# Turning half of the normalized token tiles by transposing DMAs instead of by TensorE in a hybrid decoder trunk

## The reference

```
for l in range(2):
    h = rms_norm(x, attn_pre_g[l])               # the "pre" norm
    u = h @ w_in[l]                              # 1024 -> 2560, split among four mixers
    y = concat(conv(u..), retention(u..), moba(u..), pool(u..)) @ w_out[l]
    x = x + rms_norm(y, attn_post_g[l])
    h = rms_norm(x, ffn_pre_g[l])                # the "fpre" norm
    f = silu(h @ w_gate[l]) * (h @ w_up[l])      # 1024 -> 2816, twice
    x = x + rms_norm(f @ w_down[l], ffn_post_g[l])
```

## Time and profile before

| what | us |
|---|---|
| median of 3 runs | 1102.46 (1101.63 to 1146.96) |
| the profiled execution | 1102.11 |
| its span | 1100.0 |
| PE busy | 1082.0 (98%) |
| DVE busy | 619.2 (56%) |
| ACT busy | 405.7 (37%) |
| transfers of DMA queue q1 | 31.2% of 16 engines |

### The profile page before, as it was taken

How to read it: one execution, slowest core, us unless ns; L and a number is a source line. 1 busy time by engine, 2 the same in 40 slices (tenths; PEclk the granted TensorE clock), 3 DMA queues, 4 the chain that set the end, 5 groups by cost and what they waited for, 6 DMA issues and landing times.

```text
span 1100.0 us, 15518 instructions
## 1 busy us (share of the span) xinstructions
PE 1082.0 (98%) x6086; PEld 601.9 (55%) x6086; DVE 619.2 (56%) x1419; ACT 405.7 (37%) x810; POOL 5.2 (0%) x18
## 2 busy tenths in 40 slices
PE   8999999999999999999999999999999999999997
PEld 4755784695444444444466558648844444444443
DVE  6998898873332432321568889989633433432014
ACT  5545445453332332221235463456522322321000
POOL 1000000000000000000000000000000000000000
PEclk9999999999999999999999999999999999999999
DMA  8423213254324323323013331234523333232001
GB/s 312 149 77 111 82 40 115 70 178 137 112 82 151 113 80 114 115 84 108 1 39 107 101 101 39 63 110 136 176 93 115 114 98 115 89 103 77 1 20 57
DMA packets 58167, 109.56 MB, mean 100 GB/s; under 512 B 7024, under 2 KB 7280, under 8 KB 57968
## 3 DMA queue, kind: packets, MB, share of 16 engines
q1 hardware_dynamic: 58096, 108.58, 31.2%
HBM read 106.46 MB, written 2.10 MB: 99 GB/s over the span
## 4 chain that ended last, share of the span: by engine, by line
PE 95%; DVE 3%; DMA 1%; issue 1%; ACT 0%; SPq 0%; ACTq 0%; DVEq 0%
PE ps L517 88%; PE ps L521 3%; PE ps L714 1%; PE ps L730 1%; DVE E L1302 1%; DMA xs<-x_dram 1%; PE ps L649 0%; DMA raw<-weights_dram 0%; PE ps L691 0%; PE ps L634 0%; DVE ring L1173 0%; ACT gbc L800 0%; PE ps L658 0%; PE ps L652 0%; PE ps L711 0%
## 5 line engine op out<-in xcount | busy, mean ns | idle before, releaser
L517 PE MATMUL ps<-hT,ring 128*128 128x512 f16 (+1 forms) x3264 | 547.9, 329 | 0.0
L517 PEld LDWEIGHTS ps<-hT,ring 128*128 128x128 f16 x3264 | 319.0, 98 | 223.0
L517 PE MATMUL ps<-ring,U 128*128 128x512 f16 x1440 | 313.4, 379 | 0.0
L1173 DVE SCALAR_TENSOR_TENSOR ring<-raw,ring 128x512 f16<-128x512 f32 x368 | 230.1, 684 | 80.6 <-ACT ring L800 79.8
L800 ACT ACTIVATE ring<-raw 128x512 f16<-128x512 f32 x368 | 205.5, 621 | 109.0 <-PE ps L517 78.7
L517 PEld LDWEIGHTS ps<-ring,U 128*128 128x128 f16 x1440 | 140.9, 98 | 167.0
L1497 DVE SCALAR_TENSOR_TENSOR R<-ps,R 128x512 f32<-128x512 f32 (+1 forms) x52 | 31.7, 609 | 257.6 <-ACT R L976 257.2
L517 PE MATMUL ps<-ring,hT 128*128 128x512 f16 x576 | 133.2, 383 | 0.7 <-DVE hT L1262 0.7
L976 ACT ACTIVATE R<-ps 128x512 f32<-128x512 f32 (+1 forms) x52 | 27.6, 530 | 277.9 <-PE ps L517 277.9
L1302 DVE SCALAR_TENSOR_TENSOR E<-E,par 128x256 f32<-128x256 f32 x240 | 101.9, 477 | 0.1
L517 PEld LDWEIGHTS ps<-ring,hT 128*128 128x128 f16 x576 | 56.2, 99 | 62.0 <-issue 3.0
(11 more groups left out here) (109 smaller groups left out, 494.9 us busy)
## 6 DMA issues: line engine op xcount, KB each, us to landing
raw<-weights_dram SPq DMA_DIRECT2D x368, 256.0 KB, 3.3
gbc<-gains_dram SPq DMA_DIRECT2D x8, 512.0 KB, 5.5
xs<-x_dram SPq DMA_DIRECT2D x4, 512.0 KB, 6.6
U<-weights_dram SPq DMA_DIRECT2D x8, 256.0 KB, 7.6
out_dram<-xs SPq DMA_DIRECT2D x8, 256.0 KB, 2.0
cst<-consts_dram SPq DMA_DIRECT2D x1, 1296.0 KB, 12.3
bd<-pool_w_dram SPq DMA_DIRECT2D x8, 16.0 KB, 10.1
par<-params_dram SPq DMA_DIRECT2D x1, 76.0 KB, 6.1
```

Source lines behind the costliest of these rows:

```text
L517: ins = mm(dst, st, mv_, start=first and i == 0, stop=last and i == 2, **kw)
L1173: V.scalar_tensor_tensor(out=ring[:, slot % RING, 1, raw_part(part)], in0=raw_home(n)[0], scalar=W_SCALE, in1=ring[:, slot % RING, 0, raw_ ...
```

## The change

For tiles 2 and 3 of the last three norms (fpre of layer 0, pre and fpre of layer 1) `norm_x` writes into the PSUM pair of the tile, ACT and DVE write both halves to SBUF with tokens still on the partitions, and SP issues two transposing DMAs, one for each half (128x1024 fp16 into 128x8x128), once both are there. Tiles 0 and 1, and all of pre of layer 0, stay as they were. SP issues them behind the last weight part of a slot that `HT_AFTER` names (20 counts from the start of the program; layer 1 begins at 47). PE waits for the DMAs where it waited for `h_lo`. The halves lie in the two `xn` buffers (fpre) or in `R` (pre). The table `AT` and the orders of ACT and DVE are new throughout both layers.

```diff
     {
-        ("pre_T", 2): 11, ("pre_T", 3): 38, ("moba_T", 0): 49, ("moba_T", 1): 62, ("moba_stage", 0): 76,
...
-        ("ret_Y", 0): 213, ("ret_O", 2): 217, ("ret_S", 3): 217, ("ret_O", 3): 220, ("conv_T", 1): 220,
-        ("conv_Y", 1): 231, ("pool_Y", 1): 237, ("ret_Y", 1): 257, ("fpre_T", 0): 279, ("fpre_T", 1): 280,
-        ("fpre_T", 2): 337, ("fpre_T", 3): 340, ("pre_T", 0): 852, ("pre_T", 1): 868,
...
+        ("ret_O", 3): 212, ("conv_T", 1): 212, ("pool_Y", 0): 215, ("conv_Y", 1): 227, ("pool_Y", 1): 242,
+        ("ret_Y", 1): 251, ("fpre_T", 0): 265, ("fpre_T", 1): 282, ("pre_T", 0): 852, ("pre_T", 1): 868,
     },
 ]
+HT_AFTER = {
+    ("fpre", 0, 2): 20,
+    ("fpre", 0, 3): 20,
+    ("pre", 1, 2): 50,
+    ("pre", 1, 3): 51,
+    ("fpre", 1, 2): 67,
+    ("fpre", 1, 3): 67,
+}
...
+        xsplit = {"fpre": [x_.bitcast(F16) for x_ in xn], "pre": [R[:, DM * i:DM * (i + 1)].bitcast(F16) for i in range(2)]}
...
+        def by_pe(kind, l, t):
+            return t < 2 or (kind, l) == ("pre", 0)
...
+            def h_T_load(kind, l, t):
+                sp.wait_ge(h_hi, xno(kind, l, t) + 1)
+                sp.wait_ge(h_lo, xno(kind, l, t) + 1)
+                for half_, src in enumerate((xh(kind, t), xl(kind, t))):
+                    sp.dma_start(hT[:, half_, :, tok(t)], src, transpose=True).then_inc(hT_in[t], 16)
...
+                for (kind, i, t), slot in HT_AFTER.items():
+                    if n == PARTS * (slot + 1) - 1:
+                        h_T_load(kind, i, t)
...
+            def h_ready(kind, l, tiles):
+                for t in tiles:
+                    if by_pe(kind, l, t):
+                        pe.wait_ge(h_lo, xno(kind, l, t) + 1)
+                    else:
+                        pe.wait_ge(hT_in[t], hT_no(kind, l, t))
...
-                act.wait_ge(hT_ps, xno(kind, l, t) + 1)
-                copy(hT[:, 0, :, tok(t)], pair(t).rearrange("p (k t) -> p k t", k=KT),
-                     A_SCALE / RN).then_inc(h_hi, 1)
+                if by_pe(kind, l, t):
+                    act.wait_ge(hT_ps, hno(kind, l, t) + 1)
+                    copy(hT[:, 0, :, tok(t)], pair(t).rearrange("p (k t) -> p k t", k=KT),
+                         A_SCALE / RN).then_inc(h_hi, 1)
+                    return
+                act.wait_ge(xn_sb, xno(kind, l, t) + 1)
+                xh_free(act, kind, l, t)
+                copy(xh(kind, t), pair(t), A_SCALE / RN).then_inc(h_hi, 1)
...
+                xh_free(dve, kind, l, t)
+                V.scalar_tensor_tensor(out=xl(kind, t), in0=pair(t), scalar=A_SCALE / RN, in1=xh(kind, t), op0=ALU.mult,
                                        op1=ALU.subtract).then_inc(h_lo, 1)
```

The order of DVE at the end of a layer's output stage and the start of gate and up, as a diff of its calls (the same in both layers):

```diff
                 lo_of(ybuf, pool_hi, 6, l, 1, A_SCALE, pool_y)
+                norm_x("fpre", l, 0)
                 lo_of(rz, ret_hi, 2, l, 1, 0.5 * A_SCALE * UNSCALE, ret_y)
                 norm_y("post", l, 1)
-                norm_x("fpre", l, 0)
+                split_lo(z + 17)
                 norm_x("fpre", l, 1)
-                split_lo(z + 17)
+                norm_y("post", l, 2)
                 h_lo_of("fpre", l, 0)
                 h_lo_of("fpre", l, 1)
-                norm_y("post", l, 2)
+                norm_x("fpre", l, 2)
+                split_lo(z + 18)
                 norm_y("post", l, 3)
-                split_lo(z + 18)
-                norm_x("fpre", l, 2)
                 split_lo(z + 19)
+                h_lo_of("fpre", l, 2)
                 norm_x("fpre", l, 3)
+                h_lo_of("fpre", l, 3)
+                hidden_steps(l, 0, 1)
                 split_lo(z + 20)
-                hidden_steps(l, 0, 1)
-                h_lo_of("fpre", l, 2)
-                h_lo_of("fpre", l, 3)
                 split_lo(z + 21)
```

More of the change, by code:

```diff
@@ L126 @@
     {
[L127 to L131, removed]
@@ L307, in trunk_program @@
         hT_ps = sem("hT_ps")
+        hT_in = [sem(f"hT_in{t}") for t in range(NT)]
         h_hi = sem("h_hi")
@@ L532, in last_read, with norm_done @@
                         RG: (ret_g, hs(l, s))}[slot]
+            def h_ready(kind, l, tiles):
+                for t in tiles:
+                    if by_pe(kind, l, t):
+                        pe.wait_ge(h_lo, xno(kind, l, t) + 1)
+                    else:
+                        pe.wait_ge(hT_in[t], hT_no(kind, l, t))
+            def norm_done(kind, l, t):
+                if t > 1:
+                    if kind == "post":
+                        return h_lo, xno("fpre", l, t) + 1
+                    if l + 1 < L:
+                        return h_lo, xno("pre", l + 1, t) + 1
+                return x_upd, yno(kind, l, t) + 1
             def unit(l, i, between):
@@ L546, in unit @@
                 if pre == "fpre":
-                    pe.wait_ge(h_lo, xno(pre, l, tiles[-1]) + 1)
+                    h_ready(pre, l, tiles)
                 if slot in PAIRS:
                     if pre:
-                        pe.wait_ge(h_lo, xno(pre, l, t) + 1)
+                        h_ready(pre, l, tiles)
                     take(i % 4, *pair_read(l, slot, t))
@@ L754, in small_products @@
             def small_products(l, at):
-                for t in (2, 3):
-                    if at == AT[l]["pre_T", t]: h_T("pre", l, t)
+                if l == 0:
+                    for t in (2, 3):
+                        if at == AT[l]["pre_T", t]: h_T("pre", l, t)
                 for s in range(2):
@@ L772, in small_products @@
                     if at == AT[l]["moba_Y", s]: moba_Y(l, s)
-                for t in TILES:
+                for t in (0, 1):
                     if at == AT[l]["fpre_T", t]: h_T("fpre", l, t)
@@ L1360, in ret_rotate @@
                     dve.wait_ge(retO_ps, ts(l, t) - 2)
+                if t == 0:
+                    for i in (2, 3) if l else ():
+                        dve.wait_ge(hT_in[i], hT_no("pre", l, i))
                 u = tile_bank(RQ, t).rearrange("p (a h d) -> p a h d", h=2, d=32)
@@ L1370, in moba_rotate @@
                 if t == 0:
-                    dve.wait_ge(hT_ps, xno("pre", l, NT - 2) + 1)
+                    dve.wait_ge(hT_ps, hno("pre", l, 0 if l else 2) + 1)
                     dve.wait_ge(consts_in, 16)
@@ L1630, in _ @@
                 ret_mask(l, 3)
-                conv(l, 1, 2)
-                lo_of(ybuf, pool_hi, 6, l, 0, A_SCALE, pool_y)
+                gate(l, 0)
                 conv(l, 1, 2 * CW)
@@ L1636, in _ @@
                 lo_of(rz, ret_hi, 2, l, 0, 0.5 * A_SCALE * UNSCALE, ret_y)
+                lo_of(ybuf, pool_hi, 6, l, 0, A_SCALE, pool_y)
                 pool_windows(l, 1)
```

225 lines of the change are left out of this document (123 added, 102 removed).

## The result

| kernel | median (lowest to highest, runs), us | profiled execution | its span |
|---|---|---|---|
| before | 1101.86 (1101.17 to 1146.96, 20) | 1102.11 | 1100.0 |
| changed | 1103.88 (1100.90 to 1107.06, 20) | 1103.24 | 1101.3 |

The ratio of the changed kernel to the one before is 1.0018, with a 95% interval of 1.0010 to 1.0027. I forecast 1101, so 1.1 us under the profiled time of before. It became some 2 us slower. That is far inside 2%, but it is a difference, and its sign is the other one. I had taken 22 us for what a measurement of this kernel tells from no change; the interval is about 1 us to either side. Apart from one outlier the runs of before lie within 2.1 us; those of the change spread over 6.2 us. The eleven longest of them carry a lower mean granted clock of TensorE (0.992 to 0.995) than the five shortest (0.997 to 0.999).

The account below looks back on a forecast made before the run. The prediction took PE, busy 98% of the span, as the bound. Terms -5.2 + 0.7 + 0.1 + 2.2 + 0 + 1.0 = -1.2 us gave a forecast of 1101 us, range 1096 to 1125 us.

Parts of the forecast that it names:

- Same work in other places: Small products asked for earlier by `AT`, such as `conv_T` of the second half: new PE waits, +1.0 us, bounds -3 to +4.
- the removal: Six turns of a tile leave PE at 0.87 us each: -5.2 us.
- the DMAs: Transposing pairs land 3.8 us after issue starts (0.47 + 3.3); PE waits 1.1 us per fpre norm, +2.2 together; pre 0.
- The rivals of 3 us and 6 us a DMA: Each transposing DMA fills the queue for 3 us (1114 us, chance 0.22) or 6.0 us (1150 us, chance 0.16).
- block by block: Rival: each DMA does its eight 128x128 blocks in turn, 2.0 us each, 16 us a DMA: 1270 us, chance 0.04.
- the waits at gate and up: PE waits for `h_lo` of tiles 0 and 1, +0.7 (layer 0) and +0.1 (layer 1), and for fpre DMAs, +2.2 us.
- Nothing that could have gone earlier is held back.: Weights behind the fpre transposes: slot 21 waits for slot 20's split anyway and is first used over 50 us later, 0 us.

Follow-up runs that it names:

- the products set apart: The change with slot 51 loaded ahead of the pre transposes, plus four ticks of `ret_O` and `conv_T` moved by 1 to 4: 1099.68 us, ratio 0.9979 to before.
- the two pairs of kernels with and without DMAs: The change against itself with all turns on PE (1103.88, 1110.31 us); before's input stages, hidden step and `lo_of` ahead, against the same without DMAs (1102.70, 1106.92).
- before's orders: The kernel before's ticks and ACT and DVE lists, with the transposing DMAs added and slot 51 loaded ahead of the pre transposes: 1115.34 us, ratio 1.0125.
- before's input stages: The change with slot 51 ahead, but ticks and ACT and DVE orders of both input stages from before: 1101.35 us; with second hidden step ahead of slot 21's split, 1100.03.
- the last kernel: The products set apart, plus the second hidden step ahead of the split of slot 21 on ACT and DVE: 1097.80 us, ratio 0.9970 to before.

## Why the prediction was wrong

**The step that failed** is the last term, "Same work in other places", which I set at +1.0 us within -3 to +4. With all turns left on PE, the new orders measured +8.2 (6.3 to 9.8 by the interval), twice the upper bound, and that alone turned the sign. I had looked for it at `conv_T`, the one product whose wait showed in the rows of before, and asked whether DVE keeps pace. The loss stands in other places. In the profile with all turns on PE it is 5.5 us in layer 1's input stage, where the waits are for ACT in the moba mixer (1.42 and 0.62 us) and for DVE's mask at `ret_O` (1.33), and 1.4 and 1.9 in the stretches with the hidden step (waits of 1.24 and 1.72). The wait at `ret_O` isn't a matter of DVE's pace: `ret_S` and `ret_O` at one tick leave no PE work behind which the mask could hide, and with the products set apart the kernel is 2.5 us faster. `AT` of the change has both at 212, and I read the table for ticks that moved, not for pairs that fell together. The waits at the moba products and at the hidden step I hadn't looked for at all, and for the moba products no run tries a cure. Nor did I price a lower clock behind short waits: 2.9 us at 1.2 GHz in the profile of the change. I had a row for a lower clock (0.73 at the end of the span) and used it only for long waits.

**Right: the removal.** -5.2 us: 1.75 measured for the two turns of the stretch from gate and up to layer 1, and 6.4 and 4.2 for all six by the two pairs of kernels with and without DMAs, which hold other waits too.

**Right in its mechanism, near in size: the DMAs.** I took 3.3 us to landing and measured 3.3. The Trainium skill says that transposing DMAs are as fast as regular ones ("Advanced Engine Details and Errata", section "X-Bar Transpose (TRN2)"). For the landing the trace agrees, 3.3 against 3.3 for a weight part; for the share of the 16 engines it doesn't, 1.8 us against 0.76 by my estimates. The issue is 1.3 us and not 0.47. A pair is 1.3 + 3.3 = 4.6 us and not 3.8; where SP has to issue four in a row, as with before's orders, it is 6.1 us of wait on PE. The rivals of 3 us and 6 us a DMA fall with the 1.8 us measured, and block by block with it: eight blocks land in 3.3 us together.

**Wrong, with little weight: the waits at gate and up.** I forecast 0.7 + 0.1 for the low halves and 2.2 for the DMAs, and there were none. My list of DVE's calls was near in length (20.5 us by my sum, 19.6 in the trace), but I let it start at 189.76 as before. It starts at 187.27 in layer 0: ACT's new list has the affine step of retention ahead of a square for which ACT waits for PE, where before it stood behind. So everything further on is 3 to 4 us sooner: tile 3's low half is ready at 224.7, forecast for 228.7. In layer 1 that half is ready at 766.9, no sooner than my 766.5; there it was enough that PE itself came later, at 771.5 and not at 769.2. That is luck and not my reckoning. These errors hid a part of the failed term: 1.0 was 8.2, but 3.0 was 0.

**Wrong in words, small in size: "Nothing that could have gone earlier is held back."** At fpre this holds for slot 21's first use, and yet the hidden step of DVE stands behind that slot's split and PE waits for it (0.31 us in the profile of the change, 2.46 in another). At pre, slot 51 is issued at 568 us where it could have been by 517, and ACT idles for it. The run with 51 in place of 50 is 1.7 us faster, within noise. I judged both by what PE reads from the weights and not by what ACT and DVE do behind them.

The terms: -5.2 for the turns, +8.2 for the orders, and -1.2 as the remainder, which makes +1.8 where the medians say +2.0. This is no check of the terms. The remainder isn't measured by itself: it is what the DMAs give back beyond the turns (6.4 - 5.2), so waits that go with the turns, less what slot 51 costs.

What stays open: by how much the shift of slot 51's weights, the mask waits and the clock overlap in one run, and what decides whether the clock falls behind the same waits. The edits were stacked (-1.7 for slot 51, -2.5 for the products set apart, -1.9 for the hidden step) and each was measured on the one before, not alone. Only the -2.5 is clear of noise by the ratios. The hidden step was worth nothing on the change's own ticks and 1.3 on before's input stages.

## What to carry to other kernels

When work leaves the busiest engine and a hand-written order is redone at the same time, run the new order with the old work first. Here that one run showed a loss of 8 us under a gain of 6. In a table of ticks, look for producers and consumers on the same tick, since another engine's step must lie between them. The kernel before had nine matmuls of 256 columns there and 0.14 us of idle time; with 2.1 us of work between, the last kernel has none. Allow for a short idle time on TensorE to cost more than its length in some executions, and compare two profiles of the same order before blaming a wait for it. Judge a queued DMA by how long it holds the queue's engine for the work of all engines, not only of the one that reads its data.

## What the runs showed of the hardware that I had not expected

- A transposing DMA of 128x1024 fp16 from SBUF to SBUF lands in 3.3 us like a weight part of the same 256 KB. It has 1056 packets, takes about 1.8 us of the 16 DMA engines by the estimate above and holds SP for 1.3 us, 2.6 times a weight part.
- Waits on PE of 0.40, 1.33 and 0.56 us within 5 us were followed by matmuls at 1.2 GHz, with 0.80 and 0.86 granted over 20 us, and equal work cost 2.9 us more. In another execution waits of 0.40, 1.33 and 0.57 us in the same order left the clock at 1.00. After 6.12 us of idle time the window behind has 0.64.
- The spread between runs of one kernel seems to come from two things. The change's runs lie 6.2 us apart and the longer ones have the lower clock, 0.992 to 0.995. The kernel with before's input stages lies 4.6 us apart at 0.996 to 0.999, where the clock says little, and within 0.9 us once the hidden step no longer stands behind a late weight.
